# A context norm moved ahead of cross attention, a last tile split moved, and three identity products added

## The reference, cut to what matters

```python
# first block: cross attention, then the experts
h = h + _memory_cross_attention(_rmsnorm(h, norm_xattn[l]), _rmsnorm(mem, norm_mem[l]), w_xq[l], w_xkv[l], w_xo[l])
h = h + _hierarchical_moe(_rmsnorm(h, norm_ffn[l]), ...)          # 16 experts, gate/up 1024x256, down 256x1024
...
# second block, layer l = 0: the context's norm is what the change moves
hx = modulate(rmsnorm(x, norm1_g[l]), sh1, sc1)
hc = modulate(rmsnorm(ctx, norm1_g[l]), csh1, csc1)
```

## Time and profile before

| | |
|---|---|
| median of 3 runs | 1598.14 us (1597.01 to 1600.53) |
| the profiled execution: its time, its span | 1599.01 us, 1597.3 us |
| busy: PE, DVE, ACT, POOL | 1519.0, 890.7, 710.8, 133.6 us |
| mean granted clock of TensorE | 0.975 of full speed |
| matmuls | 9875 |
| read from HBM | 239.71 MB, 151 GB/s over the span |

### The profile page before, as it was taken

The page is one execution under the profiler, slowest core; times in us unless marked ns, Lnnn a source line. Parts: engine busy times, 40 slices in busy tenths (PEclk is TensorE's granted clock), DMA queues, the critical chain, the costliest instruction groups (busy, mean ns, idle before and its releaser), DMA issues.

```text
span 1597.3 us, 23555 instructions
## 1 busy us (share of the span) xinstructions
PE 1519.0 (95%) x9875; PEld 1283.1 (80%) x9875; DVE 890.7 (56%) x1249; ACT 710.8 (44%) x1071; POOL 133.6 (8%) x157
## 2 busy tenths in 40 slices
PE   7999999988999899988899999999999998899998
PEld 6986997877787688645678888888878966799998
DVE  4633763567777749777364233233247868455554
ACT  5526543256665444466333212212235447453434
POOL 3001000010000126300200000000002410000000
PEclk9999999999999999989999999999998999999999
DMA  9477558587999342500533223233263340545552
GB/s 305 143 254 243 179 172 277 184 273 230 254 283 305 80 158 93 171 1 1 99 113 106 89 95 106 92 93 99 86 176 98 123 159 1 159 159 185 185 172 66
DMA packets 228945, 242.28 MB, mean 152 GB/s; under 512 B 13096, under 2 KB 222472, under 8 KB 228712
## 3 DMA queue, kind: packets, MB, share of 16 engines
q1 hardware_dynamic: 226704, 238.19, 46.8%
q0 software_dynamic: 1600, 2.37, 2.2%
q10 hardware_dynamic: 536, 0.22, 0.1%
HBM read 239.71 MB, written 1.05 MB: 151 GB/s over the span
## 4 chain that ended last, share of the span: by engine, by line
PE 84%; DVE 8%; ACT 4%; issue 2%; DMA 1%; ACTq 0%; DVEq 0%; SPq 0%
PE bank L802 19%; PE bank L804 18%; PE bank L803 18%; PE score_banks L1289 2%; PE bank L1944 2%; PE bank L1951 2%; PE bank L1323 2%; PE bank L1947 2%; DVE w_lo L791 2%; DVE small L1364 2%; PE bank L875 1%; PE score_banks L910 1%; PE bank L876 1%; PE bank L877 1%; PE bank L1306 1%
## 5 line engine op out<-in xcount | busy, mean ns | idle before, releaser
L791 DVE TENSOR_TENSOR w_lo<-raw,w_hi 128x2048 fp32r<-128x2048 f32 (+1 forms) x144 | 330.2, 2295 | 215.4 <-ACT w_hi L779 214.6
L802 PE MATMUL bank<-xn_hi,w_hi 128*128 128x256 f32 (+1 forms) x1232 | 407.2, 331 | 5.1 <-ACT proj L1775 2.9
L804 PE MATMUL bank<-xn_hi,w_lo 128*128 128x256 f32 (+1 forms) x1232 | 404.2, 328 | 0.0
L803 PE MATMUL bank<-xn_lo,w_hi 128*128 128x256 f32 (+1 forms) x1232 | 404.1, 328 | 0.0
L779 ACT ACTIVATE w_hi<-raw 128x2048 fp32r<-128x2048 f32 (+1 forms) x144 | 271.4, 1886 | 132.7 <-PE bank L804 96.1
L802 PEld LDWEIGHTS bank<-xn_hi,w_hi 128*128 128x128 f32 x1232 | 235.6, 191 | 27.0 <-issue 4.4
L803 PEld LDWEIGHTS bank<-xn_lo,w_hi 128*128 128x128 f32 x1232 | 235.6, 191 | 19.9
L804 PEld LDWEIGHTS bank<-xn_hi,w_lo 128*128 128x128 f32 x1232 | 235.5, 191 | 19.9
L802 PE MATMUL bank<-hid_hi,w_hi 128*128 128x256 f32 (+1 forms) x416 | 137.5, 330 | 2.6 <-DVE hid_lo L1857 1.9
L803 PE MATMUL bank<-hid_lo,w_hi 128*128 128x256 f32 (+1 forms) x416 | 136.4, 328 | 0.0
L804 PE MATMUL bank<-hid_hi,w_lo 128*128 128x256 f32 (+1 forms) x416 | 136.4, 328 | 0.0
(11 more groups left out here) (448 smaller groups left out, 2525.7 us busy)
## 6 DMA issues: line engine op xcount, KB each, us to landing
raw<-in_w_ada SPq DMA_DIRECT2D x48, 1024.0 KB, 6.0
raw<-in_w_in SPq DMA_DIRECT2D x30, 1024.0 KB, 6.4
raw<-in_w_gate SPq DMA_DIRECT2D x22, 1024.0 KB, 5.4
raw<-in_w_up SPq DMA_DIRECT2D x22, 1024.0 KB, 5.4
raw<-in_w_exp_down SPq DMA_DIRECT2D x16, 1024.0 KB, 7.7
raw<-in_w_down SPq DMA_DIRECT2D x16, 1024.0 KB, 5.2
raw<-in_w_out SPq DMA_DIRECT2D x12, 1024.0 KB, 5.3
raw<-in_w_exp_up SPq DMA_DIRECT2D x12, 1024.0 KB, 8.1
```

Source lines behind the costliest of these rows:

```text
L791: dve.tensor_tensor(w_lo[:, raw_slot[r], 0:k * cols], raw[:, raw_slot[r], 0:k * cols], w_hi[:, high_slot[name], 0:k * cols].bitcast(F32), ...
L802: pe.matmul(o, s_hi, m_hi, start=i == 0, stop=False)
L803: pe.matmul(o, s_hi, m_lo, start=False, stop=False)
L804: last = pe.matmul(o, s_lo, m_hi, start=False, stop=i == n - 1)
```

## The change

The norm `("n1", 0, 1)` moves out of the expert stage: its squares stand on ACT behind the split of the last query tile, its gains and sums on DVE ahead of the scaling of query tile 1, its moment on PE between query tiles 2 and 3 (in another bank, 5 and not 7), its guess and high parts on ACT ahead of the lambda exponent, its scaling on DVE ahead of the scaling of query tile 3, and its low parts on DVE in units 1 and 2 of cross attention. No table is loaded for it any more. The picks are transposed in pass 4 and not 6. The last down tile is split alone; the tile behind it is split after the last hidden part. Ahead of pass 0 PE does three products of the identity with itself (`pe_keep`, L1178), into a bank that nobody reads then, between the wait for the gathered tokens and the wait for the pair's low half. What the norm computes stays the same.

```diff
-        norms = [("mix",), ("mem",), ("fox",), ("sb",), ("xattn",), ("ffn",), ("n1", 0, 1)]
+        norms = [("mix",), ("mem",), ("fox",), ("sb",), ("xattn",), ("n1", 0, 1), ("ffn",)]
...
-        CONTEXT_MOMENT = bank[7][:, S:2 * S]
+        CONTEXT_MOMENT = bank[5][:, 0:S]
...
-        def dve_norm_low(dve, name):
+        def dve_norm_low(dve, name, parts=(0, 1)):
             spec = norm_spec(name)
             hi, lo = spec["out"]
-            for i, (c0, c1) in enumerate(halves(spec["n"])):
+            for i, (c0, c1) in list(enumerate(halves(spec["n"])))[parts[0]:parts[-1] + 1]:
...
-            last.then_inc(*xn_ready.mark(name))
+            if c1 == spec["n"]:
+                last.then_inc(*xn_ready.mark(name))
...
                 if c == 0 and p == 0:
                     pe.wait_ge(*gathered_high.at(KC - 1))
                     pe.wait_ge(*gathered_low.at(KC - 1))
+                    pe_keep(pe, bank[1][:, :], 3)
...
                 if j == 0:
                     pe_norm(pe, ("xattn",))
+                if j == 2:
+                    pe_norm(pe, ("n1", 0, 1))
...
-                if p == 5:
+                if p == 4:
                     pe.wait_ge(*ada_done.at(ada_batch(*ada_planned("gap", 7)[-1])))
-                    pe_norm(pe, ("n1", 0, 1))
-                if p == 6:
-                    pe.wait_ge(*rstd_ready.at(("n1", 0, 1)))
                     pe_picks_turned(pe)
...
             act_guess(act, ("xattn",))
             for j in range(1, 4):
                 act_feed(act, ("xq", j))
-
+                if j == 1:
+                    act_norm_squares(act, ("n1", 0, 1), [])
+            act_guess(act, ("n1", 0, 1), CONTEXT_MOMENT)
+            act_norm_high(act, ("n1", 0, 1))
...
-                    if p == 5:
-                        act_tables(act, ACT_EXP_LN)
-                        act_guess(act, ("n1", 0, 1), CONTEXT_MOMENT)
-                        act_tables(act, ACT_SILU)
...
-                        act_feed(act, ("down", e), 1 if e == EXPERTS - 1 else 0)
-                if p == 3:
-                    act_norm_squares(act, ("n1", 0, 1), [])
-                if p == 6:
+                        act_feed(act, ("down", e), 0)
+                if p == 4:
                     act_picks(act)
-                    act_norm_high(act, ("n1", 0, 1))
...
             for j in range(4):
                 dve_feed(dve, ("xq", j))
+                if j == 1:
+                    amps(0, 0)
+                    dve_norm_sum(dve, ("n1", 0, 1))
+                if j == 3:
+                    dve_norm_scale(dve, ("n1", 0, 1))
                 dve_scaled(dve, ("xq", j), xq[:, 2 * j:2 * j + 2, :], 256 ** -0.5)
...
                 dve_ada(dve, ada_planned("cross", i - 2))
+                if i in (1, 2):
+                    dve_norm_low(dve, ("n1", 0, 1), (i - 1,))
...
-                    if p == 5:
-                        dve_norm_scale(dve, ("n1", 0, 1))
...
-                        dve_feed(dve, ("down", e), 1 if e == EXPERTS - 1 else 0)
+                        dve_feed(dve, ("down", e), 0)
...
-                if p == 4:
-                    amps(0, 0)
-                    dve_norm_sum(dve, ("n1", 0, 1))
-                if p == 6:
-                    dve_norm_low(dve, ("n1", 0, 1))
...
+            dve_feed(dve, ("down", EXPERTS - 1), 1)
             dve_y_low(dve, 2)
```

More of the change, by code:

```diff
@@ L952, in ada_planned, with act_norm_squares @@
             return ADA_PLAN.get((phase, step), [])
-        def act_norm_squares(act, name, after, parts=(0, 1)):
+        def act_norm_squares(act, name, after):
             spec = norm_spec(name)
@@ L961, in act_norm_squares @@
                 act.wait_ge(*moment_ready.at(norm_before[name]))
-            for i, (c0, c1) in list(enumerate(halves(spec["n"])))[parts[0]:parts[-1] + 1]:
+            for i, (c0, c1) in enumerate(halves(spec["n"])):
                 act.activation(sq[:, c0:c1, :], spec["src"][:, c0:c1, :], ACT.Square)\
```

## The result

The changed kernel takes 1584.0 us (median of 4, 1582.65 to 1584.32) against 1597.58 before: ratio 0.9918, 95% interval 0.9905 to 0.9931, 13.6 us less. The forecast was 1584. Six more executions beside the experiments gave 1584.8 (1580.5 to 1587.2) against 1597.99, ratio 0.9918 again (0.9899 to 0.9937). The profiled execution took 1582.65.

A forecast was written before the change was run, and what follows sets the result against it. TensorE, busy 1519.0 of 1597.3 us, was taken as the bound, so gains come where it idles or runs at lower clock. Terms 6.6 + 3.8 + 3.1 + 1.5 - 0.6 = 14.4 us gave 1584, range 1580 to 1591.

The forecast's parts named there:

- A: Pass 5: without TensorE's 4.47 us wait for the norm's sum and the lower clock behind it, 6.6 us gained.
- B: Pass 7: norm's high and low parts no longer delay pass 6's hidden parts; 2.3 us pause plus 1.5 clock, 3.8 us.
- The picks: Expert stage: their transposes, copy and wait for the last adaptive batch move one or two passes ahead, costing the same there.
- C: Last down pass: one split ahead instead of two; 2.2 us less waiting plus 0.9 from the clock, 3.1 us gained.
- D: Ahead of pass 0: three identity products leave a 1.3 us pause and keep full clock, 1.5 us gained.
- E: Query tiles: the norm in its new place makes cross attention start later, charged 0.6 us, ends 0.3 and 1.5.
- Rival 4: Ahead of cross attention: the norm's chain stands exposed in TensorE's way, costing 16.5 us, time 1600; chance 0.03.
- Rival 2: Expert stage: loads, or ScalarE and VectorE at seams, become the bound, returning 4 to 8 us, 1588 to 1592; chance 0.20.

The follow-up runs named there:

- two reorders: Norm back in the expert stage of the changed kernel, its sum either one pass earlier (1594.5 us) or ahead of the down tile's split in pass 4 (1591.4 us).
- norm-back run: Changed kernel with the norm put back in the expert stage, last-tile split and identity products kept: 1596.4 us, ratio 0.9992 to the kernel before.
- product behind tile 3: Changed kernel with the norm's product on TensorE one query tile later, behind tile 3 instead of tile 2: 1593.2 us, ratio 0.9972.
- both splits first: Changed kernel with the old order: last down tile and next layer's tile both split ahead of the last hidden part; 1590.1 us, ratio 0.9937.
- the reorder: Norm back in the expert stage of the changed kernel, with VectorE's amps and sum ahead of the down tile's split in pass 4: 1591.4 us, ratio 0.9958.
- four loads under way: Changed kernel with four expert loads under way at a time instead of three (LOADS_AHEAD = 4): 1583.9 us, ratio 0.9918.
- the sum a pass earlier: Norm back in the expert stage of the changed kernel, with squares, amps and sum one pass earlier, product still in pass 5: 1594.5 us, ratio 0.9975.

## Why the prediction was right

The number and the sum held, and each term was within 0.25 us on the profiled pair (14.5 us by the terms measured, 14.4 by those predicted). That the median came out at 1584.0 exactly is luck: the kernel's own executions range from 1580.5 to 1587.2 us, and the profiled pair gained 1.65 us at a place that the sum didn't have.

- **A**: 6.7 measured, 6.6 predicted, and nothing new in pass 5: the gated product and the hidden part of pass 4 found their cover. But "the norm's sum" was too narrow a name for the cause. The two reorders show that with the sum out of the way the scale takes its place as the late step; 6.6 us come only when the whole norm leaves the queue.
- **B**: 4.0 measured, 3.8 predicted. 2.3 us are the pause and sure; the rest is the clock behind it, which the norm-back run did not pay at the same pause.
- **The picks** cost 0.67 us in pass 4, as said; that they cost the same less in pass 6 is taken over from there and not read by itself.
- **C**: 3.0 measured, 3.1 predicted. The pass took 4.4 us (512.27 to the next matmul at 516.70), near the 4.29 that the prediction took from B's pause. But that is one outcome of several: of eleven profiles with this pause unfilled at 2.1 us, five show 4.4 us, two 4.0, and four, at full clock, 3.0, where C is 4.6. The price of 0.9 us between the two ends was met on the profiled pair by luck of the execution. The splits moved behind it were covered, as said.
- **D**: 1.29 measured, 1.5 predicted. The pause is 1.46 us where I had 1.3, and the second half starts at 334.52, just behind its split (334.47), as I said.
- **E**: 0.50 measured, 0.6 predicted. The first maximum on DVE is 1.1 us later against the first query tile, of which PE sees nothing, as said. Rival 4's price, an exposed chain, was of the right kind: 7.3 us when it was exposed behind tile 3.
- **Not predicted**: 1.65 us from the start of pass 17. PE waits 2.68 us there and waited 2.92 before, but before the clock was low behind it and now it is 1.00 (480.10 to 483.00 above). With B and C this is the same thing: pauses of 2.1 to 2.9 us with the lower clock behind them in one execution and not in another. It is one reason why the profiled pair is 16.4 us apart and the medians 13.2 to 13.6.
- **Rival 2** did not happen in the changed kernel's two profiles: PE waits for nothing above 0.3 us from the start of pass 0 to the start of pass 17, in spite of 11 us gained, and the wait there did not grow (2.68 and 2.85 us, 2.92 before). The loads kept up as they are issued earlier too, at a DMA share of 0.91 around pass 5 and 1.00 around pass 7. The margin is thin: the run with the product behind tile 3 has a wait of 1.61 us at the start of pass 10, and over all profiles the wait at pass 17 goes up to 3.58 us. The Trainium skill (DMA: Bandwidth & Descriptors, the table at its head) gives about 358 GB/s as HBM's limit for one core, by which the time would have come back as waits for weights. This case shows 374 GB/s from 480.10 to 483.00, above that figure, and no such wait that was not there before.

Left open: why the clock falls behind a 2.1 to 2.9 us pause in one execution and not in the next; only that it does both was shown. Open too is why the stretch from layer 0 to layer 1 differs by up to 7 us between executions, and why the medians of both splits first (5.3 us) and of the reorder (5.0) show more than the expert stage of their traces (2.9 and 1.1). A single half of the norm (scale in the query tiles, high and low parts left behind) wasn't tried.

## What to carry to other kernels

A step that stands in the queue of two busy helpers costs the bounding engine more than once: take its wait away and the next part of the same step is late, so look for a stretch where all of its parts lie beside other work, and check with the chain (product, Newton, scale) that they end before they are wanted. The wait of 4.3 us ahead of TensorE's work was worth filling with products until 1.5 us were left (1.3 to 1.9 us in the trace), and products that ran over its end gave 1.4 us of it back; at a pause of 2.1 us the gain did not show in a median. Price the lower clock behind a short pause as a chance, with both outcomes beside it: here it was paid or not, by execution.

## What the runs showed that was not expected

- The same pause of 2.14 us (last down pass) had clock 0.55 behind it in the changed kernel's two profiles (first 3.8 us) and 1.00 with four loads under way, with the norm left out, with one product and with the sum a pass earlier, where nothing near it differs.
- The length of a pause did not decide it either: at the start of pass 17 the clock stayed up behind 2.68, 2.85, 2.90 and 3.02 us and fell behind 2.81, 2.84 and 2.86 us, in different profiles.
- One identity product ahead of pass 0 moved the clock's fall by 1.2 us into the pass and did not prevent it: 3.18 us of pause were left.
- Identity products cost 0.9 us each in a row (1.88 us for two, 2.84 for three, 5.42 for six), not the 1.10 us of a single one.
- Two executions of one program shifted by 6.5 us against each other within 110 us (1211 to 1321), 700 us behind the last changed instruction; one of them has a stretch of 11 us at clock 0.53 there, the other 1.00.
